# Two attention layers of a two-block model: token and memory pairs in one pipeline, normalised by tile

## The reference

```python
def windowed_gqa(q, k, v, sink):           # layer 0, 12 query heads on 4 key heads
    ...
    s = s - slopes * dist.astype(jnp.float32)[None, None, None]
    s = jnp.where(allowed[None, None, None], s, NEG_INF)
    ...
    p = jax.nn.softmax(jnp.concatenate([s, sink_col], axis=-1), axis=-1)[..., :-1]

def neighbourhood_attn(q, k, v, rpb):      # layer 1, 12 heads
    ...
    bias = rpb.astype(jnp.float32)[:, dr_idx][:, :, :, dc_idx]
    ...
    s = s + bias[None]
    s = jnp.where(in_win[None, None, None, :, None, :], s, NEG_INF)

def memory_attn(q, k, v):                  # 4 heads in both layers, into 256 memory tokens
    s = jnp.einsum('bshd,bmhd->bhsm', q, k).astype(jnp.float32) * (D ** -0.5)
    p = jax.nn.softmax(s, axis=-1)

def first_block(...):
    for i in range(DEPTH):
        ...
        x = x + jnp.concatenate([y_tok, y_mem], axis=-1) @ w_out[i]
        ...
        x = x + (jax.nn.silu(gu[..., :D_FF]) * gu[..., D_FF:]) @ w_down[i]
```

## Time and profile before

| | |
|---|---|
| median of 3 runs (lowest to highest) | 2709.09 us (2707.14 to 2709.68) |
| span of the profiled execution | 2705.2 us |
| PE / PEld busy | 96% / 83% |
| POOL, ACT, DVE busy | 45%, 36%, 35% |
| chain that ended last, by engine | PE 90%, DVE 4%, ACT 3%, issue 2%, POOL 1% |
| chain, by line | L1238 76%, next L1513 3%, L1426 2% |

### The profile page before, as it was taken

How to read it: one execution, slowest core, us unless ns; L and a number is a source line. 1 busy time by engine, 2 the same in 40 slices (tenths; PEclk the granted TensorE clock), 3 DMA queues, 4 the chain that set the end, 5 groups by cost and what they waited for, 6 DMA issues and landing times.

```text
span 2705.2 us, 46485 instructions
## 1 busy us (share of the span) xinstructions
PE 2589.5 (96%) x16378; PEld 2245.8 (83%) x16378; DVE 935.7 (35%) x1714; ACT 964.4 (36%) x2169; POOL 1222.9 (45%) x1032
## 2 busy tenths in 40 slices
PE   7989999999998999999998888999999888999999
PEld 7767888888766888888998878999999766998897
DVE  4263221222153321226733443441432443442341
ACT  4384322232285322234223223321233465322231
POOL 4554444444573444444423544444444443444443
PEclk9999999999999999999988998999999999999999
DMA  4222222222240222222211001222222100222222
GB/s 166 82 48 70 93 103 83 93 101 86 90 80 24 93 96 94 89 105 90 86 63 47 1 16 55 91 99 82 86 100 79 40 25 26 92 93 101 86 99 95
DMA packets 80491, 212.96 MB, mean 79 GB/s; under 512 B 30336, under 2 KB 33024, under 8 KB 80384
## 3 DMA queue, kind: packets, MB, share of 16 engines
q1 hardware_dynamic: 80384, 211.56, 23.4%
HBM read 209.44 MB, written 2.10 MB: 78 GB/s over the span
## 4 chain that ended last, share of the span: by engine, by line
PE 90%; DVE 4%; ACT 3%; issue 2%; POOL 1%; DMA 0%; DVEq 0%; POOLq 0%; ACTq 0%; SPq 0%
PE ps L1238 76%; PE ps L1513 3%; PE ps L1426 2%; PE ps L1408 1%; DVE s_sb L1690 1%; PE ps L1357 1%; PE ps L1385 1%; PE ps L1370 1%; PE ps L1253 1%; ACT s_sb L915 1%; PE ps L1483 1%; POOL bias_sb L663 1%; DVE s_sb L1665 0%; PE ps L1433 0%; DVE y_sb L1665 0%
## 5 line engine op out<-in xcount | busy, mean ns | idle before, releaser
L575 POOL TENSOR_TENSOR w_lo<-raw,w_hi 128x512 fp32r<-128x512 f32 (+1 forms) x704 | 977.8, 1410 | 1175.4 <-ACT w_hi L816 1175.0
L816 ACT ACTIVATE w_hi<-raw 128x512 fp32r<-128x512 f32 (+1 forms) x704 | 426.9, 653 | 1341.6 <-PE ps L1238 1323.4
L1238 PE MATMUL ps<-h_hi,w_hi 128*128 128x512 f32 (+2 forms) x2992 | 855.0, 333 | 13.5 <-POOL h_lo L747 8.1
L1238 PE MATMUL ps<-h_lo,w_hi 128*128 128x512 f32 (+2 forms) x2992 | 853.0, 332 | 0.0
L1238 PE MATMUL ps<-h_hi,w_lo 128*128 128x512 f32 (+2 forms) x2992 | 851.1, 332 | 0.0
L1238 PEld LDWEIGHTS ps<-h_hi,w_hi 128*128 128x128 f32 x2992 | 511.1, 189 | 74.7 <-issue 15.0
L1238 PEld LDWEIGHTS ps<-h_lo,w_hi 128*128 128x128 f32 x2992 | 507.0, 189 | 55.1 <-issue 1.0
L1238 PEld LDWEIGHTS ps<-h_hi,w_lo 128*128 128x128 f32 x2992 | 507.5, 189 | 54.2
L1238 PE MATMUL ps<-act_lo,w_hi 128*128 128x512 f32 (+1 forms) x880 | 280.5, 351 | 0.0
L1238 PE MATMUL ps<-act_hi,w_lo 128*128 128x512 f32 (+1 forms) x880 | 279.8, 350 | 0.0
L1238 PE MATMUL ps<-act_hi,w_hi 128*128 128x512 f32 (+1 forms) x880 | 278.8, 349 | 0.0
(11 more groups left out here) (248 smaller groups left out, 2625.7 us busy)
## 6 DMA issues: line engine op xcount, KB each, us to landing
raw<-slabs_d SPq DMA_DIRECT2D x288, 512.0 KB, 3.2
raw<-slabs_d SPq DMA_DIRECT2D x64, 704.0 KB, 4.0
rpb_raw<-rpb_d SPq DMA_DIRECT2D x24, 224.0 KB, 5.0
bias_sb<-alibi_d SPq DMA_DIRECT2D x6, 384.0 KB, 3.8
x<-x_d SPq DMA_DIRECT2D x1, 2048.0 KB, 12.7
out_d<-x SPq DMA_DIRECT2D x8, 256.0 KB, 4.7
mem_in<-mem_d SPq DMA_DIRECT2D x1, 1024.0 KB, 8.6
dn_cst<-dn_consts_d SPq DMA_DIRECT2D x1, 512.0 KB, 4.8
```

Of the source, the lines that this page charges most:

```text
L575: nc.gpsimd.tensor_tensor(w_lo[:, s, a * P:b * P], raw[:, s, a * P:b * P], w_hi[:, s, a * P:b * P].bitcast(f32), ALU.subtract).then_inc(lo ...
L816: nc.scalar.activation(w_hi[:, s, a * P:b * P], raw[:, s, a * P:b * P], ACT.Copy)\
L1238: last = nc.tensor.matmul(ps[:, s * 2 * BANK + po:s * 2 * BANK + po + n], w[:, s, wk], a[:, k, to:to + n], start=(k == 0 and w is w_hi and ...
```

## The change

1. The two `att` stages of a layer become one stage `tiles` of 8 tiles with 4 pairs each (`TilePair`, `over_tile_pairs`, `attend_tiles` on each engine): after the last token pair the first memory pair follows as the next step.
2. In it, four things are done once a tile and no longer once a pair: `move_y` and `y_hi` on ACT (128x512), the normalising product on DVE (128x512), `y_lo` on POOL; the four transpositions of the reciprocals stand in a row on PE, two tiles late; values of a tile fill one PSUM bank.
3. The spread of the reciprocals moves from ACT to DVE (a broadcast copy behind the reciprocal), in the mixed stage too.
4. The position bias of layer 1 is laid out with its mask on the host; one DMA a tile writes it to `bias_sb`. `rpb_raw`, the mask and POOL's additions are gone. The first bias load now stands behind the slabs that the projection starts with.
5. `out` of layers 0 and 1 waits tile by tile in its first slab.

```diff
 # SP
-                    src = d["rpb"]
-                    off = (2 * i + h) * (RPB_R * RPB_W) + (1 - r) * RPB_W
-                    sp.dma_start(rpb_raw[64 * r:64 * r + 64, h, :, :],
-                                 bass.AP(src.tensor, off, [[1, GRID], [RPB_W, RPB_R - 1], [1, GRID]]))\
-                        .then_inc(rpb_full, 16)
+                sp.dma_start(bias_sb[:, i % 2, :, 0:width], d[st.bias][i]).then_inc(bias_full[st.bias], 16)
...
 # POOL
-                    nc.gpsimd.tensor_tensor(
-                        bias_sb[:, i % 2, h, :].rearrange("p (r c) -> p r c", c=GRID), rpb_raw[:, h, :, ::-1],
-                        grid_mask.unsqueeze(1).to_broadcast([P, RPB_R - 1, GRID]), ALU.add)\
-                        .then_inc(rpb_masked, 1)
+                with pool.Fori(3, st.nt) as i:
+                    stage(i)
+                    y_lo(i - 3)
+                for i in range(st.nt, TILES):
+                    stage(i, i - st.nt)
+                    y_lo(i - 3)
...
 # ACT
-                    if p.back(1).exists:
-                        spread(p.back(1))
...
+                def step(p):
+                    for h in range(2):
+                        if p.after(1):
+                            turned(p.back(1), h)
+                        probs(p, h)
+                    if p.b == 3 and p.after(4):
+                        move_y(p.tile - 1, 1 - p.tile_slot)
+                    if p.b == 2 and p.after(8):
+                        y_hi(p.tile - 2, p.tile_slot)
...
 # PE
+                def reciprocals(tile, s):
+
+                    pe.wait_ge(inv_ready, tile + (st.unit0 + 1))
+                    pe.wait_ge(y_moved, tile + (st.unit0 + 1))
+                    for b in range(4):
+                        last = nc.tensor.transpose(bank(6 + s)[:, b * P:(b + 1) * P], p_rec[:, s, b, :], ident)
+                    last.then_inc(rec_done, 1)
+
+                def step(p):
+                    scores(p)
+                    if p.after(2):
+                        turn(p.back(2))
+                    if p.after(3):
+                        values(p.back(3))
+                    if p.b == 0 and p.after(8):
+                        reciprocals(p.tile - 2, p.tile_slot)
...
+                    if st.blk == 1:
+                        slab(q0, 0, st.blk, *outputs(st), made=y_lo_ready, at=st.unit0 - TILES)
...
 # DVE, mixed stage
-                    recip(p_inv[0:p.nq, p.slot, :], p_sum[0:p.nq, p.slot, :]).then_inc(inv_ready, 1)
+                    recip(p_inv[p.inv], p_sum[p.inv])
+                    copy(p_rec[p.inv].rearrange("p (h n) -> p h n", h=2),
+                         p_inv[p.inv].unsqueeze(2).to_broadcast([p.nq, 2, HD])).then_inc(inv_ready, 1)
...
 # DVE, tiles
+                        if p.b == 0 and p.tile >= 1:
+                            invert(p.tile - 1, 1 - p.tile_slot)
+                        if p.b == 1 and p.tile >= 2:
+                            normalise(p.tile - 2, p.tile_slot)
```

More of the change, by code:

```diff
@@ L77, in plan @@
     out = []
-    c = dict(slab=0, pair=0, tile=0, tn=0, ffn=0, col=0, val=0)
+    c = dict(slab=0, pair=0, tile=0, unit=0, tn=0, ffn=0, col=0, val=0)
     kinds, norms = [], []
@@ L101, in att, with tiles @@
     def att(**kw):
-        s = add("att", **kw)
+        add("att", **kw)
         c["pair"] += kw["nt"] * len(kw["blocks"])
         c["tile"] += kw["nt"]
+        c["unit"] += kw["nt"] * len(kw["blocks"])
+    def tiles(**kw):
+        add("tiles", nt=6, mem_blocks=m_blocks, **kw)
+        c["pair"] += 4 * TILES
+        c["tile"] += TILES
+        c["unit"] += TILES
     def tail(gain, blk, layer, conv, following, mixed=False):
@@ L137, in plan @@
     out[-1].queries = (0, 1, 2, 4)
-    att(nt=6, blocks=a_blocks, bias="alibi", sink=0, qt=0, kt=6, group=3, y=0, layer=0)
-    att(nt=2, blocks=m_blocks, bias=None, sink=None, qt=8, kt=0, group=1, y=6, layer=0)
+    tiles(blocks=a_blocks, bias="alibi", sink=0, kt=6, group=3, layer=0, mem_qt=8)
     tail(2, 1, 0, False, (3, 1))
@@ L143, in plan @@
     out[-1].queries = (0, 1, 2, 6)
-    att(nt=6, blocks=n_blocks, bias="rpb", sink=None, qt=0, kt=6, group=1, y=0, layer=1)
-    att(nt=2, blocks=m_blocks, bias=None, sink=None, qt=12, kt=0, group=1, y=6, layer=1)
+    tiles(blocks=n_blocks, bias="rpb", sink=None, kt=6, group=1, layer=1, mem_qt=12)
     tail(4, 1, 1, False, (6, 2, True))
@@ L706, in attend @@
[L706 to L716 removed]
+                    k = i * nb + b
+                    pool.wait_ge(y_hi_ready, k + st.unit0 + 1)
@@ L797, in _ @@
                     stream(st.slab0 + st.nf + st.nv)
+                if st.kind == "tiles":
+                    attend_tiles(st)
                 if st.kind == "att":
-                    nxt = stages[n + 1] if stages[n + 1].kind == "att" else None
-                    before = next(t for t in reversed(stages[:n]) if t.kind in ("proj", "att"))
-                    attend(st, nxt, before.nv)
+                    attend(st)
             stream(n_slabs)
@@ new lines, in sink_columns, with biased @@
+            def sink_columns(p):
+                sink = neg_sinks[p.st.sink][:, bass.ds(2 * p.tile, 2)].unsqueeze(2)
+                tt(s_sb[:, p.slot, :, 0:1], sink, sink, ALU.max)
+            def biased(p, h, bias, scale):
+                first, nq = 3e38, p.c["nq"]
+                if p.st.sink is not None:
+                    first = neg_sinks[p.st.sink][0:nq, bass.ds(2 * p.tile + h, 1)]
+                add_least(s_sb[0:nq, p.slot, h, 1:1 + p.n], bank(p.halves[h])[0:nq, 0:p.n], bias, scale, first,
+                          n_max[0:nq, p.slot, h:h + 1]).then_inc(max_ready, 1)
@@ L1850, in scores @@
+            def attend(st):
+                masks = {"meta": meta_mask, "first": first_mask, "band": band_mask}
+                def scores(p):
+                    wait(pt_done, 2 * p.count - 2)
+                    sink_columns(p)
                     wait(s_done, p.count + 1)
                     for h in range(2):
-                        first = 3e38
-                        if st.sink is not None:
-                            first = neg_sinks[st.sink][0:p.nq, bass.ds(2 * p.tile + h, 1)]
@@ L1875, in step @@
                         normalise(p.back(3))
-                    if st.mixed and p.b == 3 and p.tile < MIXED:
+                    if p.b == 3 and p.tile < MIXED:
                         w = Hidden(st, p.tile)
```

605 lines of the change are left out of this document (311 added, 294 removed).

## The result

The changed kernel takes **2722.68 us** (median of 21 runs, 2717.46 to 2736.82) against 2709.09; the ratio on record for all runs is **1.0044** (95% interval 1.0034 to 1.0055; the two medians alone give 1.0050). Forecast were 2708.9 us and a range up to 2719.0: the time lies above the range, on the side of rival 1. The kernel before has such a spread too: 14 of its 103 runs here and beside the experiments took 2717 to 2737 us, at a mean granted clock of 0.964 to 0.974 where it is on record, for some 0.98 in most others.

What follows compares the result with a forecast made beforehand. TensorE, busy 96% of the span, was taken as the bound. Layer 0 -0.1, layer 1 -3.6 and mixed attention +3.5 sum to -0.2 us on the median of 2709.09: forecast 2708.9 us (chance 0.42), range 2698.0 to 2719.0.

Steps and rivals of the forecast that it cites:

- rival 1: Ten new PE waits: the clock falls, 1.7 us each; half falling gives 2717 us, all 2725; chance 0.24.
- The new wait: PE's reciprocal transpositions, once a tile: PE stands for ACT's y_moved, 1.69 us in layer 1, 1.3 then 1.7 in layer 0.
- The gap of 0.13: PE's switch from value products to scores in each pair: taken to idle 0.13 us, making a layer 1 pair 3.07.
- rival 2: PE's value-to-score switch is free (-5.2 us) and the mixed stage's DVE copy hidden (-3.5): 2700 us; chance 0.30.
- the tile of layer 1: Layer 1, four pairs: a step of 5.29 us with the wait plus 3 x 3.07, together 14.5 us.
- Pairs 8 to 23 with the seam: Token pairs up to the memory pairs: 43.6 us in layer 0 (-1.1), 58.0 in layer 1 (-5.9).
- The first tiles: Tiles 0 and 1 of layers 0 and 1: no reciprocals yet, so -0.7 us in each layer.
- The memory pairs to out: First memory pair to first out product: 29.95 us in layer 0 (+3.4), 31.0 in layer 1 (+4.7).
- The 8.35 from the last pair to out: Layer 0, last memory pair to first out product: about 8.35 us, from 8.9 before, without the 2.13 wait.
- The clock at out: Out slabs of layers 0 and 1: the clock no longer falls after a 2.13 us idle, -1.7 us each.
- The copy in the mixed stage: Third layer: the reciprocals' broadcast on DVE delays the normalising product, +3.5 us, bounds -2 to +6.
- Rival 3: Seam before the memory pairs: tiles 6 and 7 staged late on POOL, so the seam stays; 2721.7 us; chance 0.04.

Runs made afterwards that it cites:

- first profile: Profiled execution of the changed kernel as it is, nothing altered, the longest of its runs: span 2735.0 us; the kernel's median is 2722.68 us.
- second profile: The changed kernel run again as it is, nothing altered, profiled at 2717.9 us: median 2723.62 us, ratio 1.0064 to the kernel before.

## Why the prediction was wrong, step by step

- **The new wait** (1.69 in layer 1; 1.3 and 1.7 in layer 0): right, 1.69; 1.19 and 1.48. In layer 0 the 512-wide rounding delays ACT by 0.2 to 0.3, less than the 0.4 taken.
- **The gap of 0.13**: wrong, it is 0 (pairs at 2.94). The first half of rival 2 was right, and with it the tile of layer 1 is 14.1 us and not 14.5. The Trainium skill ("TensorEngine Tiling (Array Packing)", Key Properties) has a change of tiling mode drain the array; no price of it shows at this switch either. In layer 0 tiles are 10.66 (145.17 to 155.83) for 10.6 and 11.0.
- **Pairs 8 to 23 with the seam**: 43.73 for 43.6; 60.79 for 58.0, and 57.57 in the run with full clock (products in the memory pairs): the difference is two falls. The first tiles, -0.7 each, gave -0.6 and -1.4 in the first profile.
- **The memory pairs to out**: 30.55 and 31.99 at full clock (same run) for 29.95 and 31.0; 34.96 and 32.48 as they ran. The waits at the end of layer 0 are 1.53 (for 0.4, y_moved of tile 6), none (for 1.1, the copies of the last pair) and 0.78 (for 0.7, y_moved of tile 7) at full clock; the sum is nearly that of the forecast, the parts are not. The 8.35 from the last pair to out does not follow from its terms, which give 8.9 - 2.13 + 0.4 + 1.1 + 0.7 = 8.97; it measured 8.70.
- **The clock at out**, -1.7 each: right. The first products of out have a clock of 1.00 (220 to 222 us), and from out in layer 0 to the first pair of layer 1 it is 528.59 us instead of 530.13.
- **The copy in the mixed stage**, +3.5 (bounds to +6): 4.9 with a clock near that of before (169.45 less 164.59, at 0.95 and 0.96), inside the bounds; 13.7 and 23.3 as it ran.
- **The step that failed** is the one that was put as rival 1, at 0.24: "the clock falls in the new waits". It was made a rival and left out of the sum, which thus took PE's clock to be the same in the tiles and in the mixed stage as before. Its ground was two rows, 1.32 without a fall and 1.68 with one. The trace of before had shown a fall after less, in its mixed stage, PE's wait first and then the windows:

```profile
2133.54 0.77 PE L1385 MATMUL ps<-cst,s_sb 128*128 128x128 f32 x4 [1.11 <-DVE y_sb L1665]
2132.00:2134.00 2.00, 0.89 (x11) 0.68 (x12) 1.01 (x6) 2.00 (x9) 0.22 (x1) 0.97 0.00 0
2134.00:2136.00 2.00, 2.00 (x8) 1.37 (x6) 0.62 (x5) 1.34 (x5) 0.00 (x0) 0.50 0.00 0
```

  Where rival 1 stood, its place was too narrow. It was worked out for the ten waits at the reciprocals, at 1.7 each, with PE at full work in between. There it came true in part (after two of five waits of 1.69 in either profile). But two more places lost more: the memory pairs of layer 0, where PE waits some 0.6 us in most pairs and the fallen clock stayed down for 24 and 20 us, and the last two mixed tiles, at half clock for 58 and 31 us. The mixed stage took 13.7 and 23.3 us more than before instead of 3.5. With PE kept at work in its waits the changed kernel takes 2710.72 us, near the forecast. A fall's price was read from a place where PE works without pause and the clock is back within 4 us. Nearer rows were there: in the memory pairs of before the clock was at 0.50 from 830 us to 836, after the 1.68 of the earlier trace rows, and from 188 to 195 in layer 0. Why it stays down so long in these places is open. PE's waits alone do not explain it: once the clock is down they shrink, and PE counts as busy for 31.95 of 34.00 us in the long mixed stretch.
- **Rival 3** was wrong: PE has no wait for POOL from pair 23 to out, in either layer. Its time, by its own terms, is 2721.95 and not 2721.7; that the measured median lies beside it is chance.

## What to carry over

A change that puts a wait of one to two microseconds on TensorE has two prices: the wait, and what the clock does after it. The second is read from the stage that follows the wait; here it was large in two stages that also leave TensorE waiting at full clock, and small where it works without pause. When work is gathered by tile, put the consumer a step later than its producer's last step; that was worth 20 us here, with the normalising product moved along and all else unchanged. And an operation that moves to an engine with much idle time is not free if it lands between two operations of a chain that TensorE waits for: the 0.23 us copy alone made the kernel before 26 us slower, and taking it back out of the changed kernel gave 7.5.

## What the hardware showed that was not expected

- After a wait of 1.69 us the clock falls at times and at times not: in both profiles after two of the five equal waits in layer 1, not the same two, and after none of the waits of 1.48 in layer 0. In the kernel before it fell after a wait of 1.11.
- Once at half, the clock can stay there for 24 us (memory pairs, PE busy 1.24 to 2.00 of each 2 us) and, in the mixed stage and the beginning of out, for 58 us (2256 to 2314) and, with the mixed spread on ACT, 72 us (2241 to 2313). In these two it returned in out; in the second profile it returned within the stage, after 31 us. The long mixed stretches come in tiles that had two products of ones a pair already.
- Products whose results nobody reads, in times that were idle, took 12 to 13 us off the changed kernel and narrowed its runs (2705.8 to 2713.9 instead of 2719.6 to 2736.2), with the tiles of layer 1 as long as ever (14.08 us).
